# Six chunks of each layer's input projection as two runs of 512 and 256 columns, with the halves summed by VectorE

## The reference, cut to what matters

```python
# hybrid layer
x = x + 0.5 * swiglu(rms_norm(x, ffn1_norm), w_gate_up, w_down)
z = rms_norm(x, mix_norm) @ w_in
u, q, k, v, gl = z[:512], z[512:1024], z[1024:1536], z[1536:2048], z[2048:]   # columns
y_pool = multiscale_pool(u, pool_w, pool_scale)    # running means over 2, 4, 8, 16 tokens, minus u, times pool_w
q, k = rope(rms_norm(q)), rope(rms_norm(k))        # per head of 64
y_attn = softmax_attention(q, k, v)                # causal
x = x + (gate0 * (y_pool @ w_branch_pool) + gate1 * (y_attn @ w_branch_attn)) @ w_out
x = x + 0.5 * swiglu(rms_norm(x, ffn2_norm), ...)
# second layer
q_na, k_na, v_na, q_r, k_r, v_r, g_r, gate_a, gate_b = split(x @ w_in_2)
# windowed attention on q_na, k_na, v_na; two-way retention on rotated q_r, k_r and v_r;
# gates, output projection, layer norm, a convolutional feed-forward, layer norm
```

## Time and profile before

| | |
|---|---|
| median of 3 runs | 1954.19 us |
| profiled execution, its own time | 1954.63 us |
| its span, first to last instruction | 1952.8 us |
| TensorE matmul busy | 1940.7 us (99%), 10534 matmuls |
| VectorE busy | 1363.1 us (70%) |
| ScalarE busy | 1035.5 us (53%) |
| GpSimd busy | 164.3 us (8%) |
| mean granted TensorE clock | 0.999 of full |

### The profile page before, as it was taken

How to read it: one execution, slowest core, us unless ns; L and a number is a source line. 1 busy time by engine, 2 the same in 40 slices (tenths; PEclk the granted TensorE clock), 3 DMA queues, 4 the chain that set the end, 5 groups by cost and what they waited for, 6 DMA issues and landing times.

```text
span 1952.8 us, 27601 instructions
## 1 busy us (share of the span) xinstructions
PE 1940.7 (99%) x10534; PEld 1665.2 (85%) x10534; DVE 1363.1 (70%) x1652; ACT 1035.5 (53%) x1201; POOL 164.3 (8%) x152
## 2 busy tenths in 40 slices
PE   9999999999999999999999999999999999999998
PEld 8888978888888889788889978888888978888887
DVE  7666577666676666677666556577888666677887
ACT  6444555544454455655445554356556554456664
POOL 0000130000000003104002201040001301000000
PEclk9999999999999999999999999999999999999999
DMA  8555635455455546456555544564554554555552
GB/s 328 193 185 180 206 140 194 174 192 193 172 194 193 193 160 207 153 179 234 186 191 190 171 178 141 206 248 176 193 193 145 196 177 158 208 206 191 186 191 87
DMA packets 55132, 365.74 MB, mean 187 GB/s; under 512 B 6672, under 2 KB 7952, under 8 KB 12176
## 3 DMA queue, kind: packets, MB, share of 16 engines
q1 hardware_dynamic: 49680, 349.99, 50.2%
q0 software_dynamic: 1472, 9.44, 1.3%
q10 hardware_dynamic: 3904, 5.25, 1.0%
HBM read 359.40 MB, written 1.05 MB: 185 GB/s over the span
## 4 chain that ended last, share of the span: by engine, by line
PE 96%; DVE 2%; ACT 1%; DMA 1%; issue 0%; ACTq 0%; SPq 0%; DVEq 0%
PE gate_two L1693 12%; PE up_two L1693 12%; PE bank L1624 9%; PE bank L1625 9%; PE bank L1626 9%; PE gate_two L1624 8%; PE gate_two L1626 8%; PE gate_two L1625 8%; PE gate_two L1698 6%; PE up_two L1698 6%; PE up_two L1882 1%; PE bank L1851 1%; PE up_two L1866 1%; PE bank L2143 1%; DVE w_lo L1019 0%
## 5 line engine op out<-in xcount | busy, mean ns | idle before, releaser
L1019 DVE TENSOR_TENSOR w_lo<-raw,w_hi 128x2048 fp32r<-128x2048 f32 x318 | 735.0, 2312 | 246.4 <-ACT w_hi L569 240.8
L569 ACT ACTIVATE w_hi<-raw 128x2048 fp32r<-128x2048 f32 x322 | 614.6, 1909 | 95.2 <-PE bank L1626 65.5
L1693 PE MATMUL gate_two<-br_parts,w_hi 128*128 128x512 f32 x1056 | 266.5, 391 | 0.9 <-DVE w_lo L1206 0.8
L1693 PE MATMUL up_two<-br_parts,w_hi 128*128 128x512 f32 x1024 | 246.2, 391 | 0.0
L1693 PEld LDWEIGHTS gate_two<-br_parts,w_hi 128*128 128x128 f32 x1056 | 198.1, 188 | 43.3 <-issue 2.0
L1693 PEld LDWEIGHTS up_two<-br_parts,w_hi 128*128 128x128 f32 x1024 | 188.2, 188 | 37.0
L1624 PE MATMUL bank<-w_lo,hid_hi 128*128 128x512 f32 x480 | 187.5, 391 | 0.0
L1625 PE MATMUL bank<-w_hi,hid_lo 128*128 128x512 f32 x480 | 187.5, 391 | 0.0
L1626 PE MATMUL bank<-w_hi,hid_hi 128*128 128x512 f32 x480 | 186.7, 389 | 0.0
L1624 PE MATMUL gate_two<-w_lo,br_parts 128*128 128x512 f32 x448 | 179.6, 401 | 0.0
L1626 PE MATMUL gate_two<-w_hi,br_parts 128*128 128x512 f32 x448 | 174.8, 390 | 0.0
(11 more groups left out here) (274 smaller groups left out, 2958.8 us busy)
## 6 DMA issues: line engine op xcount, KB each, us to landing
raw<-stream SPq DMA_DIRECT2D x328, 1024.0 KB, 4.8
area<-rpb POOLq DMA_DIRECT2D x2, 1536.0 KB, 7.8
area<-rows POOLq DMA_DIRECT2D x3, 1024.0 KB, 5.1
raw<-stream SPq DMA_DIRECT2D x8, 256.0 KB, 7.4
softT<-area ACTq DMA_DIRECT2D x32, 64.0 KB, 5.2
area<-rows POOLq DMA_DIRECT2D x2, 768.0 KB, 4.7
konst<-consts SPq DMA_DIRECT2D x1, 1344.0 KB, 9.0
area<-xT ACTq DMA_DIRECT2D x4, 256.0 KB, 6.7
```

Of the source, the lines that this page charges most:

```text
L569: act.activation(w_hi[:, s, :], raw[:, s, :], ACT.Copy).then_inc(hi_ready[s], 1)
L1019: dve.tensor_tensor(w_lo[:, s, :], raw[:, s, :], w_hi[:, s, :].bitcast(F32), ALU.subtract).then_inc(lo_ready[s], 1)
L1693: pe.matmul(pair[:, f, :, :], w_hi[:, s, at:at + P], parts[:, :, k, :], start=k == 0, stop=False, skip_group_check=True)
```

## The change

- `features` becomes `halves` for six chunks of each layer: m = 0 to 3, 6 and 7 of a hybrid layer, m = 1, 2, 3, 6, 7, 8 of a second layer. The first of a hybrid layer alternates the two kinds, as its input tiles arrive one by one.
- Each such chunk fills two PSUM banks instead of one, which `qk_pairs`, `u_pairs` and `mix2_pairs` name; banks 0 and 1 become one tensor `low_two` for this.
- ScalarE copies the lower half, VectorE adds the upper one (new signals `low_part`, `pair_sum`). In hybrid layers ScalarE then squares and scales from SBUF, behind the sum; at m = 0 that is now behind `split_after`.
- `u`'s first half is handled as before at the head of VectorE's m = 6 (`pooled_input(0)`), the second at m = 7 after `softmax_scores` of head 0 instead of before it.
- In second layers `turn_halves` on ScalarE moves behind the softmax's exponentials, `turn_pairs` on VectorE behind `softmax_weights`.
- The spread of the norm's factor (`spread_factor`) moves from before the sixth k tile to between the two runs, and always to bank 3.
- The last four output transfers wait on two semaphores, one for each producing engine, instead of four.

```diff
+        low_two = ctx.enter_context(nc.psum_tensor("low_two", [P, 2, 2, T], F32))
+        qk_pairs = (gate_two, up_two, gate_two, up_two)
+        u_pairs = (up_two, low_two)
+        mix2_pairs = {1: up_two, 2: gate_two, 3: up_two, 6: low_two, 7: gate_two, 8: low_two}
...
 # ScalarE, hybrid layer
                     if m < 4:
-                        act.activation(qk[:, 2 * m:2 * m + 2, :], bank[:, :, :], ACT.Copy, scale=cur[:, col:col + 1]
-                                       ).then_inc(mix_evac.sem, 1)
-                        if m >= 2:
-                            act.wait_ge(qk_ms.sem, here.at(qk_ms, m - 1))
-                        act.activation(qk_sq[:, m % 2, :], flat(bank[:, :, :]), ACT.Square).then_inc(qk_sq_ready.sem, 1)
+                        lower_half(qk[:, 2 * m:2 * m + 2, :], qk_pairs[m]).then_inc(low_part.sem, 1)
+                    elif m in (6, 7):
+                        lower_half(u[:, 2 * (m - 6):2 * (m - 5), :], u_pairs[m - 6]).then_inc(low_part.sem, 1)
...
+                    if m < 4:
+                        act.wait_ge(pair_sum.sem, here.at(pair_sum, m + 1))
+                        act.activation(qk_sq[:, m % 2, :], flat(some), ACT.Square).then_inc(qk_sq_ready.sem, 1)
+                        act.activation(some, some, ACT.Copy, scale=cur[:, col:col + 1]).then_inc(mix_evac.sem, 1)
...
 # VectorE, hybrid layer
+                def pooled_input(n):
+                    some = u[:, 2 * n:2 * n + 2, :]
+                    dve.wait_ge(low_part.sem, here.at(low_part, n + 5))
+                    add_upper(some, u_pairs[n]).then_inc(pair_sum.sem, 1)
+                    dve.wait_ge(pair_sum.sem, here.at(pair_sum, n + 5))
+                    dve.tensor_tensor(some, some, factors, ALU.mult).then_inc(mix_scaled.sem, 1)
...
+                    if m < 4:
+                        dve.wait_ge(low_part.sem, here.at(low_part, m + 1))
+                        add_upper(qk[:, 2 * m:2 * m + 2, :], qk_pairs[m]).then_inc(pair_sum.sem, 1)
...
-                    if m in (6, 7):
-                        dve.tensor_tensor(u[:, 2 * (m - 6):2 * (m - 5), :], banks[4 + m % 2][:, :, :], factors, ALU.mult
-                                          ).then_inc(mix_scaled.sem, 1)
+                    if m == 6:
+                        pooled_input(0)
...
                         softmax_scores(here, m - 7, CAUSAL_KEYS, ...)
+                    if m == 7:
+                        pooled_input(1)
...
 # TensorE
-                        features(c, two(bank), br_hi, br_lo, DT)
+                        halves(c, qk_pairs[m] if m < 4 else u_pairs[m - 6], br_parts)
...
 # TensorE, second layer
+                    elif m in mix2_pairs:
+                        halves(m, mix2_pairs[m], br_parts)
```

More of the change, by code:

```diff
@@ L393, in hybrid_and_neighbourhood_kernel @@
         rear_hi = signal("rear_hi", 0, 1)
-        out_pair = [sem(f"out_pair{j}") for j in range(HALVES)]
+        out_pair = [sem(f"out_by_{engine}") for engine in ("scalar", "vector")]
         ln_var = signal("ln_var", 0, 2 * TT)
@@ L758, in _ @@
                         gate_out(m, 1)
-                    bank = banks[4 + m % 2]
                     if m == 0:
@@ L790, in _ @@
                         e.then_inc(qk_var_ready.sem, 1)
+                    if m < 4:
+                        col, some = C_Q if m < 2 else C_K, qk[:, 2 * m:2 * m + 2, :]
+                        act.wait_ge(pair_sum.sem, here.at(pair_sum, m + 1))
+                        if m >= 2:
+                            act.wait_ge(qk_ms.sem, here.at(qk_ms, m - 1))
+                        act.activation(qk_sq[:, m % 2, :], flat(some), ACT.Square).then_inc(qk_sq_ready.sem, 1)
+                        act.activation(some, some, ACT.Copy, scale=cur[:, col:col + 1]).then_inc(mix_evac.sem, 1)
                     if m == 10:
@@ L917, in _ @@
                         softmax_exp(here, m - 5, ALL_KEYS, lambda a: 1.0)
+                    if 6 <= m < 10:
+                        if m == 6:
+                            act.wait_ge(dist_ready.sem, here.at(dist_ready, RET_HEADS))
+                        act.wait_ge(mix_evac.sem, here.at(mix_evac, m + 1))
+                        turn_halves(here, m - 6, two)
                     if 0 <= m - 18 < RET_HEADS:
@@ L1387, in times_gain, with mix_sum @@
                             dve.scalar_tensor_tensor(out=extra, in0=bias, scalar=ALPHA, in1=extra, op0=ALU.mult, op1=ALU.add))
+                def mix_sum(m):
+                    dve.wait_ge(low_part.sem, here.at(low_part, m if m < 4 else m - 2))
+                    some = qk[:, 2 * m:2 * m + 2, :] if m < 4 else ret_qk[:, 2 * (m - 6):2 * (m - 5), :]
+                    if m == 1:
+                        e = dve.scalar_tensor_tensor(out=some, in0=mix2_pairs[m][:, :, 0, :], scalar=HEAD_DIM ** -0.5, in1=some,
+                                                     op0=ALU.mult, op1=ALU.add)
+                    else:
+                        e = add_upper(some, mix2_pairs[m])
+                    e.then_inc(mix_evac.sem, 1)
                 def head_lower(h):
@@ L1409, in _ @@
                         softmax_scores(here, m - 5, ALL_KEYS, near)
-                    if 7 <= m < 11:
-                        turn_pairs(here, m - 7, ret_qk[:, 2 * (m - 7):2 * (m - 6), :], K_COS2, K_SIN2)
+                    if 6 <= m < 9:
+                        mix_sum(m)
                     if 0 <= m - 15 < RET_HEADS:
@@ L1504, in _ @@
                         softmax_weights(here, m - 5, ALL_KEYS)
+                    if 7 <= m < 11:
+                        turn_pairs(here, m - 7, ret_qk[:, 2 * (m - 7):2 * (m - 6), :], K_COS2, K_SIN2)
                     s = m % SLOTS
@@ L1710, in halves @@
                             both(k, f)
+                    if between:
+                        between()
                     for k in range(DT):
```

74 lines of the change are left out of this document (41 added, 33 removed).

## The result

| | before | after |
|---|---|---|
| median of 19 runs of each, side by side | 1954.45 us | 1957.81 us |
| lowest to highest | 1953.95 to 1957.6 | 1954.8 to 1962.13 |
| profiled execution, its span | 1954.63, 1952.8 us | 1955.15, 1953.4 us |
| TensorE matmul busy, matmuls | 1940.7 us, 10534 | 1937.2 us, 10150 |

The ratio is 1.002, with a 95% interval of 1.0014 to 1.0026: slower by about 0.2%, which by the prediction's own bound (slower above 1958.1) counts as the same. The execution that was profiled is the second fastest of the 19; the median lies 2.7 us above it. So there are two things to explain: what the profile shows (+0.5 us), and what it doesn't (the other 2.7).

What follows compares the result with a forecast made beforehand. TensorE, busy 99% of the span, was taken as the bound. Hybrid layers + 2.35 and + 2.1 us, second layers - 2.6, gave + 1.8 on the profiled 1954.63: 1956.4 us, range 1951.5 to 1960.0.

Steps and rivals of the forecast that it cites:

- the forecast's own range: Whole kernel: 1954.1 to 1958.4 us around the forecast of 1956.4, that case given a chance of 0.50.
- The matmuls: Changed chunks on TensorE: two runs take 5.54 us instead of 5.76, saving 0.22 a chunk, 5.3 us over 24.
- Second layers: Second layers: copy and addition lie in idle time and cost nothing, so the full 2.6 us is gained.
- Front of a hybrid layer: Hybrid layer's start: waits of 0.15 us for the square and 0.3 for the norm's factor, 0.45 a layer.
- the 0.15 at m = 0: First hybrid chunk: the square, behind the sum and `split_after`, makes TensorE wait 0.15 us, bounds 0 and 0.6.
- The keys: VectorE at m = 6: swapped keys' DMA wait hides copy and addition; keys end 12.17 us behind chunk 5.
- The pooled sums: Hybrid layers: GpSimd starts 4.5 us after the keys, chain 17.95 us; TensorE goes on 2.35 and 2.1 us later.
- Nowhere else over 0.5: Sign: TensorE idles 2 to 4 us before the pool's matmuls in both hybrid layers, nowhere else over 0.5 us.
- The rival of longer waits and the clock: Pooled sums: a third split enters GpSimd's chain, or TensorE's clock falls, or both; 1958.6 to 1962 us; chance 0.22.
- The third split: VectorE's next split gets in before GpSimd's last difference: 2.2 us more in a layer, 4.4 in both.
- The other side: Rival: pooled sums in time, only gains stay, 1950.2 us, or 1953.3 with half the wait; chance 0.20.
- at the pooled sums and nowhere else: By the skill's advice on idle gaps, the clock rival's price falls due only at the pooled sums' wait.

## Why the prediction was right, and where it wasn't

The median came out 1.4 us above the forecast of 1956.4 and just inside the forecast's own range; the sum of the terms is right in kind, but one term is too dear and a rival that came true in part was left out, and these two partly cancel. The profiled execution, 1955.15, is what the terms account for; that the median lies so near the forecast is luck.

- **The matmuls.** 0.22 us a chunk forecast, 0.20 measured (5.56 against 5.76), 0.17 for the one behind scores (5.68 against 5.85). Right.
- **Second layers.** - 2.6 forecast; - 2.27 in the two profiles (the pool's matmuls of the second hybrid layer come 793.14 - 790.27 = 2.87 us later, the end of the span only 0.6) and - 2.33 with those layers changed alone. Copy and sum are hidden there. Right. The trial includes the change at the last transfers, which wasn't tried by itself.
- **Front of a hybrid layer.** 0.45 us of waits forecast; chunk 5 ends 0.55 us earlier where four chunks at 0.22 give 0.88: 0.33. No wait shows before chunk 1's end: two chunks bring 0.38 (206.59 in both, with this one 0.38 late from the start). The gain is missing at chunk 2, which takes 6.30 us (207.40 to 213.70) against 6.28 before. There the factor comes just in time: GpSimd ends it at 211.18, TensorE's spread starts at 211.23, and its weight load had waited 0.4 us for it. So the forecast wait for the factor, 0.3, is there with 0.2; the 0.15 at m = 0 is not. TensorE's and GpSimd's timelines:

```profile
213.70 0.95 PE L2039 MATMUL low_two<-konst,area 128*128 128x2 f32 x8
```

```profile
210.46 0.72 POOL L453 TENSOR_TENSOR rs<-ms,small 128x2 f32<-128x2 f32 x1 [183.33 <-ACT ms L625]
```

Queries and keys gain about 1.3 us in both layers (the trial with the pooled input as before, - 3.63, less that of second layers alone, - 2.33), forecast 8 x 0.22 - 0.9 = 0.86.
- **The keys.** "Stay 12.17 us behind the end of chunk 5" failed: 245.27 - 233.79 = 11.48. The wait of 1.69 us for the swapped keys had vanished, and VectorE went from the first multiplication straight to the keys' pairs. The four transfers were issued at the same time in both (from 234.2 before, 234.0 here), but the slowest took 7.2 us to land before and 6.5 here, and VectorE came later to them (242.46 against 241.6). The prediction had held the transfer to be as late as before. Why it was faster wasn't tried.
- **The pooled sums.** Start 4.46 us after the keys, forecast 4.5; chain 17.44, forecast 17.95; a wait in both hybrid layers and nowhere else, for GpSimd, as forecast. But it is 2.06 and 2.30 us long, not 3, and the pool's matmuls begin 0.99 us later in the first layer and 1.5 more in the second, where 2.35 and 2.1 were forecast. This is the term that was mis-sized: by 1.36 us in the first layer, of which 0.69 came from the keys, 0.51 from the chain and 0.12 from the front. The second layer's start, 774.3, is 0.1 above what the same shift gives (773.09 + 1.1). With the measured terms the sum is + 0.99 + 1.5 - 2.27 = + 0.2 instead of + 1.8; the profiled execution shows + 0.5, with 0.38 of it from its late start. These terms are read from the same two profiles, so the sum only closes the account; the trials (- 2.33, and - 3.63 without the two chunks) are the test. "Nowhere else over 0.5" holds for new waits only: those of 1.7 and 1.1 us were there before.
- **The rival of longer waits and the clock.** It was given 0.22 as a case of its own. It is no alternative but a part of the result, in some executions and not in others, and the likely source of the 2.7 us between the profiled execution and the median. The third split's part is shown: moving it away takes the upper group off, 1957.8 to 1956.9. The clock's part is less sure. Filling the wait besides takes the median to 1955.7, which is the profiled execution's 1955.15 within the difference of the runs of before (0.4), and takes executions at 0.998 or less from five of 11 to one (after has 13 of 19). But after has one profile, of its second fastest execution, and no profile here shows the clock falling behind a pool wait of 2.05 to 2.30 us: it fell behind one of 2.83, behind one of 1.88 at another place, and six times behind the wait of 1.7 us for ScalarE, which both kernels have. Its prices were near for the split (2.2 forecast, 2.1 measured) and too high for the clock (2.8 forecast, 1.6 measured; 0.7 to 1.5 at the wait for ScalarE). The closeness of median and forecast is a cancellation: pooled sums 2 us too dear in all, this rival left out at about 2.7.
- **The other side.** The forecast rated it at 0.20 because the moved addition stands behind the softmax by program order. Moving it before the scores gives just that case: no pool wait, 1951.82. The forecast for it, 1950.2, left out the wait at head 0's weights, 2 x 0.43.
- **What bias and splits cost GpSimd.** 0.98 us of GpSimd's time for 1.76 us of the gates' bias, forecast 1.15. By the Trainium skill, GPSIMD Engine Reference, section 1, instructions with two SBUF inputs contend with GpSimd's; the trial that moves the bias agrees in kind.
- **The idle time.** The Trainium skill, TensorE: Matmul & The Clock Gate, section "Why this matters for your kernels", tells to avoid idle gaps between bursts of matmuls, because they cost the clock. The rows agree after gaps of 1.88 and 2.83 us, and of 1.7 us in six profiled executions; but the profiled execution of after kept 1.00 through gaps of 1.69, 2.06 and 2.30 us. So here such a gap makes the fall possible, not certain, and "at the pooled sums and nowhere else" was wrong.

What stays open: why the same gap costs the clock in one execution and not in another, and how much of after's 2.7 us is lost behind the pool's waits and how much at the wait for ScalarE. A profile of one of after's executions above 1959 would tell.

## What to carry to other kernels

When a faster engine runs into a chain that another engine finishes just in time, price the chain, not the matmuls: nearly 5 us of saved matmul time (24 x 0.20) came back as two waits of 2.2 us, and one reordered pair of instructions (the sum before the softmax) kept most of it. Look for long instructions that start within tenths of a microsecond of a chain's end; whether they get in can differ between executions, which a single profile doesn't show, so compare the profiled execution with the median of the runs before trusting it. Where a gap can't be closed, shorten it first: with the pool's waits at 1.1 and 1.3 us none of 11 executions had a mean clock under 0.999, with 2.05 and 2.29 us five of 11 did. And before a fall of the clock is put down to a new gap, look for it behind the old ones.

## What the hardware showed that was not expected

- After a gap on TensorE the clock didn't fall in the gap but when work had been taken up again: 0.8 us after the matmuls resumed in one case (253.89, 254.7), 1.3 us in another (794.92, 796.24), 1.1 in a third (1500.49, 1501.62). It stayed at 1.2 GHz for some 3.4 us each time, which cost 1.6 us in the first case.
- The same wait of 1.69 to 1.72 us cost the clock in six of twelve profiled executions and left it at 1.00 in the other six.
- A copy of 6 columns on GpSimd took 2.32 us while VectorE split a tile, and 0.19 us for 8 columns when it didn't. A split of 2.28 us costs GpSimd about 2.1 us whatever its own work is: the sum of 248 columns 2.81 against 0.72 us, the four differences 5.93 against 3.83. The gates' bias of 1.76 us costs it 0.98.
- It works the other way too: VectorE's operation on 2 columns (L1185) took 0.16 us alone and 0.68 beside GpSimd's last difference, with which it ended.
- A float32 matmul call of 256 columns takes 0.43 us in a row of its like (3.45 / 8), and leaves two records in the trace.
